# Separate buffers for four final states, and transposes for the gathered rows, in a retention, block-attention and mixture-of-experts step

## The reference

```python
def retention_chunk(s, qkv):            # per head, chunks of 128 tokens, 4 heads, state 128 x 256
    ...
    s_new = s * jnp.exp(ld * L)[None, :, None, None] + jnp.einsum('bjhd,bjhe->bhde', k_dec, vf)
    return s_new, inner + cross
...
ret = retention_output(r_out, rg)       # group norm per head, silu gate
att = moba(...)                         # block-sparse attention, 8 heads
merged = jax.nn.sigmoid(gr) * r + jax.nn.sigmoid(ga) * a
...
def hier_moe(h, ...):                   # top-1 of 4 groups, top-2 of 8 experts in it, 32 experts
    a = jnp.einsum('bld,edf->blef', h, w_gate)
    u = jnp.einsum('bld,edf->blef', h, w_up)
    act = jax.nn.silu(a) * u * combine.astype(h.dtype)[..., None]
    return jnp.einsum('blef,efd->bld', act, w_down)
```

## Time and profile before

| | |
|---|---|
| median of 3 runs | 773.66 us (773.31 to 775.98) |
| the profiled execution's own time | 770.15 us |
| its span, first to last instruction | 768.3 us |
| mean granted TensorE clock, share of full speed | 0.933 |
| busy: PE / PEld / DVE / ACT / POOL | 694.2 / 501.4 / 282.8 / 149.0 / 100.9 us |
| moved by DMA | 242.88 MB, mean 316 GB/s |

### The profile page before, as it was taken

One profiled execution on the slowest core, in us unless ns is written; L12 is line 12 of the kernel. 1 busy time (PEld: TensorE's weight loads), 2 busy tenths in 40 slices (PEclk: granted clock), 3 DMA queues, 4 the chain that ended last, 5 costly groups with the idle time before them and its releaser, 6 DMA issues.

```text
span 768.3 us, 13775 instructions
## 1 busy us (share of the span) xinstructions
PE 694.2 (90%) x5069; PEld 501.4 (65%) x5069; DVE 282.8 (37%) x1552; ACT 149.0 (19%) x425; POOL 100.9 (13%) x136
## 2 busy tenths in 40 slices
PE   6999999799999588998998999469999999999974
PEld 4888888677888366743426877367865756666631
DVE  3004838978886576400001222614214111111103
ACT  3334323343244122200000001301101001011013
POOL 1565107400002124000000000010000000000000
PEclk9999999899999799999999999657999897999997
DMA  9948998899989689879999698837599969999981
GB/s 308 265 135 316 361 341 286 273 383 376 352 274 389 225 289 343 308 262 351 410 406 349 242 417 342 308 103 307 206 385 374 364 254 392 397 385 390 417 303 59
DMA packets 94902, 242.88 MB, mean 316 GB/s; under 512 B 8834, under 2 KB 54530, under 8 KB 86514
## 3 DMA queue, kind: packets, MB, share of 16 engines
q1 hardware_dynamic: 58050, 193.51, 66.4%
q10 hardware_dynamic: 31200, 31.39, 12.4%
q0 software_dynamic: 5584, 17.08, 6.8%
HBM read 234.88 MB, written 9.11 MB: 318 GB/s over the span
## 4 chain that ended last, share of the span: by engine, by line
PE 73%; DMA 15%; DVE 7%; ACT 2%; issue 2%; SPq 1%; ACTq 0%; DVEq 0%; POOLq 0%
PE zps L903 34%; PE nps L1188 8%; PE zps L1176 8%; PE nps L1061 5%; PE zps L1211 4%; DVE kall L1378 3%; DMA kall<-in_w_up 3%; DMA out<-rows_a 3%; DMA ring_all<-in_w_ret_o 3%; DMA gain<-v_rows 2%; PE nps L874 2%; PE bps L1226 2%; DMA hT<-in_w_down 1%; PE zps L874 1%; PE zps L1230 1%
## 5 line engine op out<-in xcount | busy, mean ns | idle before, releaser
L903 PE MATMUL zps<-hT,ring_all 128*128 128x264 f32 x1152 | 273.7, 393 | 1.6 <-DVE hT L1559 1.0
L903 PEld LDWEIGHTS zps<-hT,ring_all 128*128 128x128 f32 x1152 | 217.9, 193 | 45.3 <-issue 4.8
L1378 DVE CUSTOM_DVE_ANT_0 kall<-kall,qb 128x128 f32<-128x128 f32 x512 | 129.0, 317 | 66.1 <-DMA kall<-in_cache_k 63.5
L1176 PE MATMUL zps<-cst,rows_b 64*128 64x64 f32 x256 | 64.6, 407 | 5.1 <-DMA rows_b<-h_rows,tidx_i 5.1
L1176 PEld LDWEIGHTS zps<-cst,rows_b 64*128 64x128 f32 x256 | 62.1, 331 | 8.5 <-issue 8.5
L605 POOL DMA_INDIRECT rows_b<-h_rows,tidx_i x16 | 15.1, 941 | 373.2 <-DMA h_rows<-rows_b 194.6
L903 PE MATMUL zps<-headT,ring_all 128*128 128x264 f32 x256 | 58.5, 388 | 3.7 <-DMA ring_all<-in_w_ret_o 2.3
L903 PEld LDWEIGHTS zps<-headT,ring_all 128*128 128x128 f32 x256 | 48.2, 190 | 14.8 <-issue 4.8
L1061 PE MATMUL nps<-ring_all,zret 128*64 128x512 f32 x224 | 51.5, 599 | 2.8 <-DMA ring_all<-in_cache_v 2.8
L1378 DVE DVE_READ_ACCUMULATOR2_ANT scores<- 128x1 f32 x512 | 40.6, 79 | 0.0
L1546 DVE TENSOR_TENSOR hT<-zps,zatt 128x264 f32<-128x264 f32 x8 | 3.5, 432 | 93.1 <-PE zps L903 93.0
(11 more groups left out here) (365 smaller groups left out, 829.9 us busy)
## 6 DMA issues: line engine op xcount, KB each, us to landing
kall<-in_cache_k SPq DMA_DIRECT2D x64, 512.0 KB, 6.9
ring_all<-in_cache_v SPq DMA_DIRECT2D x56, 512.0 KB, 7.4
ring_all<-in_w_in ACTq DMA_DIRECT2D x26, 1024.0 KB, 10.8
ring_all<-in_w_gate SPq DMA_DIRECT2D x10, 1024.0 KB, 15.7
ring_all<-in_w_up SPq DMA_DIRECT2D x10, 1024.0 KB, 17.7
ring_all<-in_w_down SPq DMA_DIRECT2D x8, 1024.0 KB, 10.5
ring_all<-in_w_in SPq DMA_DIRECT2D x6, 1024.0 KB, 13.2
kall<-in_w_gate SPq DMA_DIRECT2D x5, 1024.0 KB, 8.3
```

The source lines that it names most:

```text
L903: mm = pe.matmul(zps[m % 2][:, 0:T], w[:, k, P * fb:P * (fb + 1)], rhs[:, k, :], start=(k == 0), stop=(k == KT - 1))
L1176: mm = pe.matmul(zps[0][:, 2 * CAP * k:2 * CAP * k + rows], xg[par][0:rows, k:DM:KT], ident[at, at], start=True, stop=True, tile_position= ...
L1378: ins = v.tensor_tensor_reduce(kh, kh, qb[b % 2][:, P * h:P * (h + 1)], 1.0, 0.0, ALU.mult, ALU.add, scores[:, pg, AH * b + h:AH * b + h + 1])
```

## The change

`sfin` becomes a list of four buffers of 256 columns, one for each head, in parts of `rows_a` and `rows_b`; the wait on the store goes. In `x_tr` each of the eight calls of a pair becomes a `pe.transpose` of the same strided slice, with the same identity block. Nothing is moved in any engine's list.

```diff
-        s1, sfin = rows_a[:, 512:768], rows_a[:, 768:1024]
+        s1 = rows_a[:, 512:768]
+        sfin = [rows_a[:, 0:256], rows_a[:, 256:512], rows_a[:, 768:1024], rows_b[:, 0:256]]
...
-                        act.dma_start(ret_prompt[0, 0, r], sfin[:, :]).then_inc(r_st, 16)
+                        act.dma_start(ret_prompt[0, 0, r], sfin[r]).then_inc(r_st, 16)
...
-                    mm = pe.matmul(zps[0][:, 2 * CAP * k:2 * CAP * k + rows], xg[par][0:rows, k:DM:KT], ident[at, at],
-                                   start=True, stop=True, tile_position=(2 * CAP * par, 0))
+                    mm = pe.transpose(zps[0][:, 2 * CAP * k:2 * CAP * k + rows], xg[par][0:rows, k:DM:KT], ident[at, at])
...
-                if r >= 1:
-                    v.wait_ge(r_st, 16 * r)
-                v.scalar_tensor_tensor(out=sfin[:, :], in0=s1[:, :], scalar=float(np.exp(LD[r] * P)),
+                v.scalar_tensor_tensor(out=sfin[r], in0=s1[:, :], scalar=float(np.exp(LD[r] * P)),
```

## The result

The changed kernel took 743.12 us (median of 4 runs, 741.18 to 746.31), the kernel before 773.48 beside it (4 runs, 769.08 to 775.98). The ratio is 0.9617, interval 0.9561 to 0.9674: 30.4 us less. The forecast was 741, 33 less than the 773.66 it started from. The executions that were profiled are 746.31 after (span 744.5) and 770.15 before. The first is the slowest of its kernel's four and the second on the low side, so the two profiles lie only 23.8 us apart. Whatever is read between them falls short of the medians by 6.5 us, and the first thing to settle is in which stage. Ratios leave out an execution over 1.5% above the fastest of its kernel: one of the six of the kernel that turns twice (752.89) and one of the kernel before in the third set (782.28).

The account below looks back on a forecast made before the run. It took PE as the bound up to about 700 us, with a one-time store wait and the DMA close behind. The profiled 770.15 less 9 and 24 is 737; with 3.5 for the median, 741, its own range 734 to 749.

Parts of the forecast that it names:

- Part 1: Retention: without DVE's 8.1 us wait for head 1's store, 9 us less in all, bounds 3 and 11.
- The clock's share: After the old stall: no fall of PE's granted clock, so faster projection blocks and L991, about 2 us.
- The wait is replaced: Rival, chance 0.12: sample rows and states become the pace after 255 us; the store's fix gives 3, total 747.
- Part 2, PE's price: Turning of gathered rows: eight transposes take 1.2 us a pair in place of 4.04, saving 2.8, bounds 1.7 and 3.3.
- Part 2, the release: SP's release for the first down weights, 14 us earlier than 556.10 from five pairs turned faster, at about 542.
- Part 2, the DMA as the new bound: Expert stage: PE becomes faster than 32.3 us a quad, so DMA bounds it; 24 us less, bounds 12 and 31.
- The 61 MB: Weights from expert 12 and down 7 to expert 31 and down 27: 164 us at 390 GB/s, ending near 708.
- The 27 worked out before any allowance: Expert stage's gain with the DMA as bound: expert 31's weights end near 708 in place of 735.4.
- The 3 us set aside for a slower clock and DVE's steps: Expert stage: 24 taken, not 27, for DVE and ACT before the next turning and PE's clock falling more often.
- Experts give half: Rival, chance 0.14: low clock or a dry DMA keeps a quad near 32 us; experts gain 12, total 752 to 753.
- The transposes cost what the products did: Rival, chance 0.04: the strided load is paid twice or its row half not used; total 765.
- The clock: Rival, chance 0.03: transposes leave PE's array so idle that its clock stays at 1.2 GHz through the experts; about 809, slower.

Follow-up runs that it names:

- the kernel that turns twice: The changed kernel with each of the eight transposes of a pair issued twice, 16 in place of 8: 745.87 us, ratio 0.967.
- the third set: Runs of three and of four half-row buffers for sample values, beside the changed kernel and the kernel before, whose median there was 771.91 us.
- The four-row kernel: The changed kernel with two final-state buffers and four in place of two for half rows of sample values: 734.19 us, ratio 0.9518.

## Why the prediction was right, step by step

**Part 1: 9 predicted, 8.4 measured alone.** The 8.1 us wait has gone, and PE waits 0.4 to 0.5 us ahead of L992 in three profiles (1.5 in the first). The clock's share was priced at 2. From 255 to 270 the mean granted clock was 0.66 before and is 1.00 in the first profile, as forecast, but 0.89 in two others of the same kernel. No run separates the clock's share from the wait's, so that 8.1 plus 2 less 1 came out is shown only as a sum, to some 3 us.

What would be late next was named rightly, sample rows, but priced at "nothing or a few tenths". In the first profile it was more: the wait of L978 for the update grew from 4.5 to 8.3 us and one row took 9.01 to land, over the 7.7 I had as the worst. This was the rival *The wait is replaced*, and by that profile alone it nearly held (3.9 against its 3). The other three profiles of the same kernel say otherwise: the wait of L978 was 4.8 to 6.2 there, and the worst row took 7.2 to 7.6. The first gather was issued at 496.31, 495.42 and 492.89 in them, and at 498.2 in the first. The same code thus reaches the experts within a band of 5.3 us, and the first profile was at its late end. The profile of before was at the early end of its own: its first gather is at 502.20, and the kernel with only the transposes, whose code is the same up to there, has it at 505.28. Over all profiles on record the eight without the wait on the store and with two row buffers average 495.0, the two with that wait 503.7. That is 8.7 us, where the pair of first profiles shows 4.0, so this stage holds about 4.7 of the 6.5 us by which they fall short of the medians. The four-row kernel shows where the rival has its truth: the rows were the next limit, worth 4.7 us at the first gather. What they took back of the 8.1 is too small for these runs to show.

**Part 2, PE's price: 1.2 a pair predicted, 1.02 to 1.14 measured.** PE's busy time in the turning went from 64.6 to 17.6 us. The forecast of this price was luck. The 0.243 us that it started from were already one load: 62.1 us over 256, and a product has two of them. That a transpose loads once halves the number, from 16 loads to 8, and leaves 8 x 0.243 = 1.9 us, with the pipeline's end 2.1. The prediction halved the load as well, without a row for it, and the load did halve: 15.3 us over 128 is 0.12 each, and a single one of the same 64 strided rows is listed at 201 ns in place of 331. Why it is shorter no run here tests. The Trainium skill, TensorE: Matmul & The Clock Gate, Terms, says four times faster for fp32, and here the mean is 4.04 to 1.10 us, 3.7 times. SBUF — State Buffer, Door 1, speaks of a penalty for strided reads, and one is seen in the transposes; but the prediction's reading of it, that they would cost near half a product's, did not come (1.10 is near a quarter, and even 1.2 was no half of 4.04). The same shape read contiguously (64x128, at 320 us in the changed kernel) has 138 ns:

```profile
L875 PEld LDWEIGHTS bps<-cst,zret 64*128 64x128 f32 x8 | 0.6, 138 | 0.3 <-issue 0.3
```

Little hung on it. By the prediction's own working, a price of 2.3 would have given 21 us where it took 24.

**Part 2, the release: 542 predicted, 539.0 measured.** The 542 left part 1 out. The release is 17.1 earlier, of which 3.6 were already there at the start of the stage; 13.5 against the 14 that five pairs should give. Over all four profiles of the changed kernel, against before and the kernel with only the buffers (50.4 and 50.7 us from the first turning to the release), it is 13.9.

**Part 2, the DMA as the new bound: shown.** Shares of 1.00 to 1.02 from 557 on, PE free 8 to 10 us in each of the last three, 22.5 us gone with 8.4 million bytes, 14 us more of PE for 5.

**Part 2, one size that was off.** The 61 MB from 541 end near 711 (expert 30's at 705.8 and 5.4 for the last 2 MB), which is 376 GB/s where I had 390: 6 us in 170. The DMA itself moved 385 GB/s in these 170 us, 65.5 million bytes where the weights are 64.0. So about 2 of the 6 us are the rate, and 4 are other transfers, the gathered rows among them, that the sum left out. The 27 worked out before any allowance had 14 ahead of the first release and 13 behind it. Ahead of it 13.9 came. Behind it, from the release to the last issue of down weights, it was 177.7 and 179.7 us with products and is 170.0 to 172.4 in the changed kernel: 7 to 8. Together that is some 21; 23.2 were measured alone, against the 24 taken. The 3 us set aside for a slower clock and DVE's steps are not seen as such; by chance they covered half of the 6 us that the sum of the bytes was short. The tail shifted as said: 31.9 to 34.9 us from the last issue of down weights to the end, 34.4 before.

**One thing was said too broadly:** that PE would wait for gate and up weights "in most experts". It waits eleven times, 25.3 us in all, the longest 4.3, and most experts find theirs landed.

**The rivals.** *Experts give half* needed free DMA in the windows; from 541 to 711 the share was 0.99. *The transposes cost what the products did* fell with 17.6 us. *The clock* needed a mean granted clock under 0.7; it was 0.79 in the first window and 0.85 to 1.00 in the others, lower where PE waits. The Trainium skill's Part 4 of TensorE: Matmul & The Clock Gate, by which transposes do not count as activity, is neither supported nor refuted: a transposed pair is now 1 us between products, and the window 585 to 607 with two of them stood at 1.00.

## What to carry to other kernels

When a fix shortens one engine's list, price the stage by the next limit and not by the time removed: 47 us of PE went from the turning and 23 came out, because the bytes needed the rest. A stall of one occurrence can be worth its whole length (8.1 us of wait, 8.4 measured, to some 3 us) if everything behind it is fed by the engine that stalled; then give the space that the fix could spare (two of four buffers here) to whatever waits next. When a price is halved because something is done once in place of twice, look whether the number that is halved was for one or for both. And compare several profiles of one kernel before reading a stage's difference of a few us as a mechanism.

## What was not expected of the hardware

The same program reached the expert stage at points 5.3 us apart, by when single rows and states landed (sample rows took 3.4 to 9.0 us in one profile). And SP stops being free: from 500 to 740 us, 14 of its 77 issues of weights took 2 us or more before, and 29 do now, up to 5.26; where the DMA has room they take 0.3 to 0.6. One loop is shown here, timeline of SP in the changed kernel:

```profile
616.02 2.81 SPq L453 DMA_DIRECT2D ring_all<-in_w_up  x1
618.88 1.36 SPq L457 DMA_DIRECT2D cst<-in_w_down  x1
620.28 5.11 SPq L453 DMA_DIRECT2D kall<-in_w_gate  x1
```

What stands behind such an issue in SP's list starts later: the chain of waits goes through some of them (SPq L453, 1% of the span). Whether an earlier issue would have gained anything, with the DMA at a share of 1.02, no run here tests.
